# Second layer's input projections as Strassen's seven half-size products per pair of column blocks, in a two-layer hybrid decoder on one core

## The reference

```python
def stick_breaking_branch(h, w_in, w_out):        # w_in (1024, 4096)
    proj = h @ w_in
    q, k, v, gate = jnp.split(proj, 4, axis=-1)   # 8 heads of 128
    ...
        z = jnp.einsum('bhqd,bhsd->bhqs', q_blk, k) * scale
        log_1m = jnp.where(mask, jax.nn.log_sigmoid(-z), 0.0)
        tail = lax.cumsum(log_1m, axis=3, reverse=True) - log_1m
        A = jnp.where(mask, jnp.exp(jax.nn.log_sigmoid(z) + tail), 0.0)
        return jnp.einsum('bhqs,bhsd->bhqd', A, v)
    ...
    return (o * jax.nn.silu(gate)) @ w_out
```

## Time and profile before

| what | us |
|---|---|
| three runs: lowest, median, highest | 1467.22, 1469.33, 1471.59 |
| the profiled execution | 1469.78 |
| its span in the profile | 1468.1 |
| PE busy in the span | 1386.8 |
| DVE, ACT, POOL busy in the span | 903.0, 640.1, 435.1 |

### The profile page before, as it was taken

One profiled execution on the slowest core, in us unless ns is written; L12 is line 12 of the kernel. 1 busy time (PEld: TensorE's weight loads), 2 busy tenths in 40 slices (PEclk: granted clock), 3 DMA queues, 4 the chain that ended last, 5 costly groups with the idle time before them and its releaser, 6 DMA issues.

```text
span 1468.1 us, 18492 instructions
## 1 busy us (share of the span) xinstructions
PE 1386.8 (94%) x7351; PEld 1135.2 (77%) x7351; DVE 903.0 (62%) x1540; ACT 640.1 (44%) x887; POOL 435.1 (30%) x230
## 2 busy tenths in 40 slices
PE   6898999999999999996998999999999999997896
PEld 4687788888888888885886787878787877875785
DVE  7387787869787878777338255454545555557313
ACT  6153435253535353443235354545454454546113
POOL 6542333323333343335124422111212122111120
PEclk9999999999999999997999999999999999999999
DMA  7211110101111101130111201111111111000302
GB/s 188 58 29 29 29 37 22 50 24 37 30 36 37 36 22 37 33 110 27 65 42 57 72 29 44 29 30 29 29 43 29 30 29 40 27 21 0 115 29 114
DMA packets 97190, 65.20 MB, mean 44 GB/s; under 512 B 2401, under 2 KB 91602, under 8 KB 97106
## 3 DMA queue, kind: packets, MB, share of 16 engines
q1 hardware_dynamic: 97106, 64.04, 14.7%
HBM read 53.54 MB, written 10.49 MB: 44 GB/s over the span
## 4 chain that ended last, share of the span: by engine, by line
PE 80%; DVE 12%; POOL 3%; ACT 2%; issue 2%; DMA 0%; POOLq 0%; SPq 0%; DVEq 0%; PEldq 0%; ACTq 0%
PE psum L408 51%; PE psum L1761 4%; PE psum L1787 4%; DVE terms L1316 3%; POOL acc L637 2%; PE psum L1774 2%; PE psum L1704 2%; PE psum L1649 2%; PE psum L1719 2%; PE psum L1674 2%; PE psum L1695 2%; PE psum L1658 1%; DVE small_L L1301 1%; DVE stick L1444 1%; PE psum L1600 1%
## 5 line engine op out<-in xcount | busy, mean ns | idle before, releaser
L408 PE MATMUL psum<-u_hi,w_hi 128*128 128x512 f32 x1264 | 523.9, 414 | 26.0 <-DVE u_lo L1089 7.2
L408 PE MATMUL psum<-u_lo,w_hi 128*128 128x512 f32 x1264 | 517.2, 409 | 0.0
L408 PE MATMUL psum<-u_hi,w_lo 128*128 128x512 f32 x1264 | 506.6, 401 | 0.0
L381 POOL TENSOR_TENSOR w_lo<-w_raw,w_hi 128x1024 fp32r<-128x1024 f32 (+1 forms) x83 | 213.2, 2568 | 702.8 <-ACT w_hi L376 702.8
L408 PEld LDWEIGHTS psum<-u_hi,w_hi 128*128 128x128 f32 x1264 | 240.5, 190 | 81.9 <-issue 19.7
L408 PEld LDWEIGHTS psum<-u_lo,w_hi 128*128 128x128 f32 x1264 | 240.4, 190 | 51.1 <-issue 7.5
L408 PEld LDWEIGHTS psum<-u_hi,w_lo 128*128 128x128 f32 x1264 | 240.2, 190 | 49.8 <-issue 3.8
L376 ACT ACTIVATE w_hi<-w_raw 128x1024 fp32r<-128x1024 f32 (+1 forms) x83 | 85.8, 1034 | 158.7 <-PE psum L408 103.8
L708 POOL TENSOR_TENSOR Lb<-dec,level 128x512 f32<-128x512 f32 (+1 forms) x64 | 89.0, 1406 | 126.5 <-PE psum L1704 69.2
L1185 DVE SCALAR_TENSOR_TENSOR late<-raw,cols,late 128x1024 f32<-128x1024 f32 x72 | 120.1, 1668 | 1.9
L1028 ACT ACTIVATE soft<-psum 128x1024 f32<-128x1024 f32 (+3 forms) x64 | 41.7, 652 | 154.1 <-DVE psum L1432 153.4
(11 more groups left out here) (212 smaller groups left out, 2032.5 us busy)
## 6 DMA issues: line engine op xcount, KB each, us to landing
w_raw<-in_a_w_in SPq DMA_DIRECT2D x33, 512.0 KB, 4.1
w_raw<-in_b_w_in SPq DMA_DIRECT2D x32, 512.0 KB, 4.0
x_stage<-in_x SPq DMA_DIRECT2D x8, 512.0 KB, 7.3
w_raw<-in_b_w_out SPq DMA_DIRECT2D x8, 512.0 KB, 3.6
out<-fin_o SPq DMA_DIRECT2D x8, 512.0 KB, 2.6
resid<-late SPq DMA_DIRECT2D x6, 512.0 KB, 3.4
o_rows<-o_nrm SPq DMA_DIRECT2D x12, 256.0 KB, 2.0
w_raw<-in_a_w_out SPq DMA_DIRECT2D x8, 384.0 KB, 3.2
```

The lines of the kernel that those rows point to most:

```text
L381: G.tensor_tensor(tiles(w_lo, key), tiles(w_raw, key), tiles(w_hi, key).bitcast(F32), ALU.subtract).then_inc(lo_done, 1)
L408: mm = PE.matmul(psum[:, half], (w_hi, w_hi, w_lo)[part][:, n % 2, k], (u_hi, u_lo, u_hi)[part][:, k, half * HALF:(half + 1) * HALF], star ...
```

## The change

Columns come in pairs: q with k (pair 2h), gate with v (pair 2h + 1), 16 pairs in all. Of a pair's weight, with its k blocks in two halves, and of the input, with its k blocks and its tokens in two halves, the four quarters each are combined as in Winograd's form of Strassen's algorithm: seven products p1 to p7 of half the depth instead of eight. A product is 4 k blocks x 3 parts = 12 matmuls (`GROUP`), a pair 84, a head 168 where it was 192. Four results come out of two PSUM banks that go on accumulating: a bank is read, then the next product is added to what is in it.

- **Input.** Once, between the layers, the combinations T1 to T4 of the input (16 blocks of 128x512) are made by DVE (`difference_t1`, `sums_t`) and split by ACT, POOL and DVE. The squares are now made and added in token halves.
- **Weights.** For every pair POOL makes three sums and, later, a fourth (128x512 each), and each of the seven factors is split by itself (`factor_hi`, `factor_lo`, 128x512), in a ring of four.
- **Evictions.** Of the seven products of a pair, ACT takes p1 and p2 (a copy), and DVE p6, p7, p5, p4, p3, each as an addition of the bank to a half of `b_raw`. On DVE they stand at two fixed places a step.
- **Filling.** Two places a step: between `weigh` and the second transposes, and at the end (`STEP_FILL`). Step 0 has six matmuls ahead of v's transposes (`FIRST_FILL`).
- **Memory.** All eight x blocks go to DRAM and come back at the end (two of them in the last head); each head's output goes to DRAM (`b_rows`) and is read back when the last head begins. The output weights 0 and 1 are split in steps 0 and 1 of the last head.

```diff
-STEP_FILL = ((4, 8, 6, 23), (4, 8, 5, 11), (4, 6, 4, 10), (4, 5, 3, 9), (4, 5, 0, 8), (4, 4, 0, 6),
-             (2, 1, 0, 0), (4, 4, 14, 22))
+STEP_FILL = ((12, 23), (10, 15), (9, 13), (8, 11), (0, 15), (0, 12), (0, 2), (15, 23))
+FIRST_FILL = 6
+ORDER = ("p1", "p6", "p2", "p7", "p5", "p4", "p3")
+FIRST_ORDER = ("p1", "p2", "p6", "p7", "p5", "p4", "p3")
+SECOND_BANK = ("p6", "p7", "p4")
+STARTS = ("p1", "p6", "p5")
+BY_ACT, BY_DVE = ("p1", "p2"), ("p6", "p7", "p5", "p4", "p3")
...
+        def factor_sums(p):
+            raw = raw_of(p)
+            G.wait_ge(pair_in[p % 2], 32 * (p // 2 + 1))
+            if p > 0:
+                G.wait_ge(s_lo, 7 * p - 2)
+            G.tensor_tensor(w_sum[:, 0], raw[:, 1, low], raw[:, 1, high], ALU.add).then_inc(s_made, 1)
+            G.wait_ge(s_made, 4 * p + 1)
+            G.tensor_tensor(w_sum[:, 1], w_sum[:, 0], raw[:, 0, low], ALU.subtract).then_inc(s_made, 1)
+            G.tensor_tensor(raw[:, 1, low], raw[:, 0, low], raw[:, 1, low], ALU.subtract).then_inc(s_made, 1)
...
+        def pair_products(p, first, last):
+            for m in range(first, last):
+                g, j, part = m // GROUP, m % GROUP // 3, m % 3
+                name, f = order_of(p)[g], 7 * p + g
+                if j == 0 and part == 0:
+                    PE.wait_ge(s_lo, f + 1)
+                    if name in ("p2", "p5"):
+                        PE.wait_ge(pair_act, 2 * p + (1 if name == "p2" else 2))
+                    elif name in ("p7", "p4", "p3"):
+                        PE.wait_ge(pair_dve, 5 * p + {"p7": 1, "p4": 2, "p3": 3}[name])
...
@@ SP, at the end
-            all_arrived(sp, 3)
-            for k in range(HOME, KB):
-                sp.dma_start(xT(k), resid[1, k - HOME]).then_inc(late_in, 16)
+            all_arrived(sp, 2)
+            for k in range(2, KB):
+                sp.dma_start(xT(k), resid[1, k]).then_inc(x_in[k], 16)
...
@@ ACT, between the layers
+            ended_pair(0)
+            for name in ("p4", "p3"):
+                for j in range(HALF_KB):
+                    input_hi(name, j)
+            for cb in range(HALF_KB):
+                b_square(cb, 1)
+            ended_pair(1)
...
@@ ACT, attend
                     if s == 0:
-                        take_b(h, 7)
-                    fill.to(STEP_AT[4 * s])
+                        ended_pair(14 * h + 13)
+                    fill.to(STEP_AT[2 * s])
...
+                    if not follow and s < 2:
+                        split_hi(("out", s))
...
-                    fill.to(STEP_AT[4 * s + 2])
-                fill.to(QUAD - MMS)
+                    fill.to(STEP_AT[2 * s + 1])
+                fill.to(2 * PAIR - GROUP)
...
```

517 lines of the change are left out of this document (375 added, 142 removed).

## The result

The changed kernel takes **1500.68 us** (median of 4 runs, 1498.93 to 1501.51), the kernel before 1468.54 us on the same chip (4 runs, 1467.22 to 1471.59). The ratio is 1.0214, with a 95% interval of 1.0195 to 1.0233: 32 us slower. Forecast were 1480.2 us and a range of 1447 to 1496. The direction was right, the size was not, and the time lies outside the range.

What follows compares the result with a forecast made beforehand. PE's matmuls were taken to bound the middle heads, with waits for other engines between the layers and in the last head. 1469.78 - 15.0 (heads) + 20.7 (between layers) + 1.7 (last head) + 3.0 (end) = 1480.2 us; range 1447 to 1496.

Steps and rivals of the forecast that it cites:

- The heads: Seven heads with filling: each gains 2.15 us, 15.0 us in all of the 38.1 their removed matmuls are worth.
- step 0, v's second transposes: In step 0 of a head, v's second transposes wait for DVE, which makes one more eviction first: 0.3 us.
- step 1, p5 behind p2's copy: In step 1 of a head, p5 waits for ACT's copy of p2, which stands behind silu: 1.0 us.
- step 5, scores wait for `b_k`: At step 5's end, the scan ahead of q and k's scaling can meet a POOL split: 0.4 us, between 0 and 1.2.
- steps 6 and 7: End of a head: DVE's chain up to p7's eviction takes over, 17.0 us where it was 17.08, nothing gained.
- rival C: In step 0 POOL's gate scaling wins the race against DVE's scan: 18 us more over seven heads, 1498; chance 0.18.
- Between the layers: Stage up to the first attended step: POOL's work and its contention with DVE delay that step by 20.7 us, to 880.3.
- The walk through the queues: Between the layers, operations followed queue by queue: p2 starts at 822.3, p5 839.3, p4 845.4, p3 851.7.
- The clock: Between the layers, PE's clock may fall behind its stands: nothing in the sum, 5 us in the range.
- The last head: Output weight 1's split ahead of silu and one more DVE eviction: +1.7 us, up to 4 if POOL's gate scaling meets DVE.
- The end: Output stage: output weight 2 loads behind three more x blocks, 4.8 us of which 1.8 are hidden: +3.0 us.
- A: Evictions stay hidden in all seven heads, no contention between the layers: 1447.5 us; chance 0.25 including cases towards no change.

Runs made afterwards that it cites:

- c2: Changed kernel with e1, e2, e3, e6, e7 and e5's PE order (pair 1's first group ahead of the block sum), filling dealt out anew: 1451.07 us.
- e2: Changed kernel with ScalarE's copy of p2 in step 1 moved ahead of the gate's silu: 1487.84 us.
- e1: Changed kernel with VectorE's eviction of p7 in step 7 moved ahead of the scan: 1491.60 us.
- d1: Changed kernel with GpSimd's gate scaling in step 0 moved ahead of the factor's lower part beside it: 1505.19 us.
- e5: e3 with TensorE's order between the layers moved too, block sum directly behind pair 0, and pair 1's first factor made earlier on GpSimd: 1489.90 us.
- e6: e3 with seven additions of squares between the layers moved from GpSimd to VectorE: 1489.98 us.
- e3: Changed kernel with the order between the layers changed on ScalarE, GpSimd and VectorE, TensorE's order as it was: 1500.82 us.
- c3: c2 with two moves in the last head: gate scaling directly behind the scan, output weight 1's upper part in step 2: 1451.05 us.
- e7: Changed kernel with the loads of the third and fourth output weight blocks issued ahead of the residual's: 1499.58 us.
- e4: Kernel before with the heads' filling in two places a step instead of four, no Strassen products: 1467.22 us.

## Why the prediction was wrong, point by point

**The heads (-15.0 forecast, -2.0 measured): the step that failed most.** The named waits were the right ones, but their sum of 1.7 us a head was too small, and the first head had a loss that the sum had no term for. What each step of a middle head lost against its own matmuls:

| place | forecast | measured | shown by |
|---|---|---|---|
| step 0, v's second transposes | 0.3 | 0.6 (0.31 of it a wait) | trace, c2 |
| step 1, p5 behind p2's copy | 1.0 | 1.65 | e2 |
| step 5, scores wait for `b_k` | 0.4 | 1.0 | c2 |
| steps 6 and 7 | 17.0 in all | 17.12 | e1, c2 |

Steps 0 to 5 lost 3.25 us instead of 1.7: 1.55 more in each of six heads, 9.3 us. In the seventh, whose step 5 has no wait for `b_k` (4.41 us instead of 5.42), it is 0.5. For step 1 the copy was ready as forecast (8.1 us into the step, 8.2 forecast), but PE stood there at 6.8 and not at 7.2, and 0.2 more went in starting again. In step 0 the wait was 0.31, as forecast; no wait accounts for the other 0.3. For step 5 I had named both bounds, 0 and 1.2, and chosen 0.4: the scan of 128x256 took 1.69 us (0.68 before) against a GpSimd split at 1196.93, so the upper one was near. The second piece is the first head, whose step 0 took 14.61 us instead of 11.67, +2.9: 1.2 because the race of rival C was lost there alone, and 1.8 because PE ran at a granted clock of 0.54 behind the stand of 3.36 us (d1, e5, e6). 9.3, 0.5, 2.9 and 0.3 in steps 6 and 7 are the 13.0 that were missing.

**Steps 6 and 7** went as said, to 0.1 us: the chain over softplus, sum, scan, exponent, p7's eviction let p4 start 11.26 us behind step 6 (1136.00 to 1147.26; 11.2 forecast). But I said that "nothing is gained" there, as if it were a bound; e1 shows that it was a place in a queue, and c2 that steps 6 and 7 can take 14.1 us, of which 0.9 are the four products fewer that stand there in c2.

**Between the layers (+20.7 forecast, +27.1 measured).** The walk through the queues met the trace: p2 at 822.07 (822.3 forecast), p7 832.45, p5 839.07 (839.3), p4 845.76 (845.4), p3 852.49 (851.7). The failure is in the last sentence of the sum, from p3 to the first attended step: 28.6 us forecast, 34.1 measured. Of the 5.5 missing, 3.36 are a wait for head 0's first exponent, of which the sum had no term: its scores had come so late that softplus, sum, scan (3.29 us beside GpSimd instead of 2.28) and exponent no longer fitted beside the rest of pair 1. 1.7 are the clock: p3's twelve matmuls took 4.45 us (852.49 to 856.94) for 2.7. The remaining 0.4 is spread over the matmuls behind them. The clock I had named, at 5 us in the range and nothing in the sum, "as PE waits for POOL anyway"; that holds for p7, p5 and p4, and fails for the last group in front of work that doesn't wait, and again for the scores behind the exponent's wait: with the 1.8 us in the first head that stand cost 5.2 us. The clock and this wait are the terms that were put at nothing.

e3, e5 and e6 say what the walk meant, which I had not seen: a new order of the producers alone moves nothing (e3), because PE waits for the end of GpSimd's work. Taking work off GpSimd (e6) and asking PE to wait for it at another place (e5) won 10.8 and 10.9 us.

**The last head (+1.7, measured +4.0; "up to 4" stood beside it).** Step 0 is 1.1 us longer (7.08 against 5.94), step 1 1.9 (8.69 against 6.79), the wait ahead of step 2's transposes 0.9 (4.46 against the 3.52 of the earlier trace rows). Of the 1.1, 0.4 are the wait for VectorE (3.00 against 2.62); the rest is the clock, granted at 0.50 from 1355.00 to 1357.60: in e1, with the same wait of 3.00, it was 0.88 at that place (1347.70 to 1349.00) and step 0 took 6.32 us. The 1.9 are the VectorE operation that meets GpSimd:

```profile
1357.84 2.36 POOL L958 TENSOR_TENSOR b_raw<-b_raw,rsb 128x1024 f32<-128x1024 f32 x1
```

```profile
1358.27 3.01 DVE L1406 TENSOR_TENSOR u_lo<-o_raw,u_hi 128x1024 fp32r<-128x1024 f32 x1
```

3.01 us against 1.21 before. In other runs VectorE's lower part is served sooner and its scan of 128x768 meets GpSimd (1.75 us before). In each, step 1 is longer than 6.79 us by what the two operations took more:

| run | lower part, scan | both together more | step 1 longer by |
|---|---|---|---|
| changed kernel | 3.01, 1.74 | 1.8 | 1.9 |
| e1 | 1.50, 2.85 | 1.4 | 1.5 |
| c2 | 1.58, 2.88 | 1.5 | 1.5 |
| d1 | 1.22, 2.86 | 1.1 | 1.2 |
| c3 | 2.27, 1.74 | 1.05 | 1.05 |

So in step 1 the loss is what VectorE loses beside GpSimd. The 0.9 in front of step 2 isn't the upper part of the output weight alone, as the forecast had it: e1 has that too and waits 3.35 us. There the lower part took 1.50 us, so the mask and the softplus and silu behind it came sooner.

**The end (+3.0, measured +1.6).** The wait is there and its cause is right (e7), its size is 1.35:

```profile
1414.03 0.50 PE L446 MATMUL psum<-u_hi,w_hi 128*128 128x512 f32 x1 [1.35 <-POOL w_lo L416]
```

The output weight 2 landed 14.3 us behind the first load's issue (1396.10 to 1410.40) where it was 11.05 before: 3.25 us for three blocks more, not 4.8. I took 330 GB/s for the loads; in 1400 to 1406 us they moved 386.

**Rivals.** A (evictions hidden, 1447.5) is near what c2 reaches, 1451.1, but only once their places and the filling are changed, and by another sum: 39.6 us less in the seven heads and 18.0 more between the layers, where A had 36.4 and 9.4. C was priced at 2.6 us a head; d1 made it happen and it costs 1.2, since the scan met only the second half of GpSimd's operation. C's own time, 1498, lay outside the range, though it had a chance of 0.18. The range failed because its upper end took C's price on top and left out that several terms could be at their upper bounds at once: step 1, step 5, the exponent, the clock and the last head all were.

**Open.** A head of c2 takes 60.84 us. Before, less 24 matmuls and the wait of 1.05, it would be 59.97. Of the 0.9 us between them 0.16 is the wait shown. In part it is the distance of two matmuls in a row: 0.2317 us on average in c2, 0.2301 before, 0.2285 in e4 (over more than 400 each), 0.3 us a head; what sets this distance no run shows. The rest, 0.4 us, stays open, as does what the upper part ahead of the silu costs in the last head.

## What to carry to other kernels

When a change takes work from the engine that binds, look in every step for the reader that now comes early, and put evictions and small producers directly behind the event that they need, ahead of anything long on their engine; then deal the free work out again so that no wait stands while another step has slack. Where reordering the producers' queues only moves a wait, count the work of the engine behind it: move operations off it, even if a shared port takes a third back, or let the reader do something else before it asks. Give the lower clock behind a stand a term of its own wherever the work behind it doesn't wait. Add up the upper bounds of waits that hang on the same stretch before a range is written.

## What the runs showed of the hardware that I had not expected

**A short stand costs twice.** Stands of PE of 2.1 to 3.0 us, after twelve matmuls (24 ahead of p7), were followed by a granted clock of 0.63 to 0.64, eight or nine matmuls at about 0.43 us and then 0.23; so each cost 1.6 to 1.7 us more than the stand. The stand of 3.36 us ahead of the first attended step cost 1.8 more, at 0.54. In e6 PE stood for 0.90 us ahead of 831.90 and for 1.00 us ahead of 848.20, and what followed ran at 1.00. Rows of e6 (columns as above):

```profile
831.90:837.70 5.80, 5.78 (x24) 4.40 (x24) 5.80 (x4) 0.63 (x1) 5.80 (x4) 1.00 0.00 0
839.50:844.00 4.50, 4.23 (x12) 2.86 (x12) 4.29 (x5) 1.87 (x3) 4.42 (x3) 0.66 0.29 77
844.00:847.00 3.00, 2.94 (x12) 2.33 (x12) 2.90 (x3) 0.88 (x3) 2.85 (x5) 0.94 0.89 234
848.20:853.00 4.80, 4.80 (x20) 3.74 (x21) 2.69 (x3) 1.89 (x4) 4.72 (x4) 1.00 0.00 0
```

The second follows a stand of 1.79 us, and there the clock fell in the middle of the group (0.23 us up to 840.98, 0.43 behind it). The Trainium skill's page TensorE: Matmul & The Clock Gate, section "HAM oscillation — how this bites in real kernels", tells the pattern: bursts of matmuls parted by waits for operands, each of which begins at the lower clock. The four groups at 0.63 to 0.64 agree with it; the stretches behind 0.90 and 1.00 us show stands that did not bring the lower clock.

**The race is decided by hundredths.** GpSimd's 2.38 us operation began 0.08 us ahead of the scan and cost it 2.2 us; 0.17 us behind (a middle head, 1155.35 against the scan's 1155.18) it took 4.10 us itself and the scan 2.09. In e6 it began 0.03 us behind in the first head and took 4.17, the scan 2.02. Both orders occur in one execution of one program.
